# Projection units of two k tiles instead of one between the attention's steps

## The reference, cut to what matters

```python
for l in range(DEPTH):                       # DEPTH = 2
    hn = rmsnorm(h, norm_gain[l])
    proj = hn @ w_in[l]                      # 1040 x 1024 by 1024 x 4104
    dq, dk, dv, dg, fq, fk, fv, ff, fg = jnp.split(proj, split_points, axis=-1)
    dq, dk = partial_rope(dq, cos, sin), partial_rope(dk, cos, sin)
    do = diff_attention(dq, dk, dv, lam, chunk_ids)       # softmax(map 0) - lam * softmax(map 1)
    do = rmsnorm(do, subln_gain[l], SUBLN_EPS) * (1.0 - lam_init) * silu(dg)
    fo = forgetting_attention(fq, fk, fv, cum_logf, positions) * silu(fg)
    h = h + jnp.concatenate([do, fo], axis=-1) @ w_out[l]
```

## Time and profile before

| what | us |
|---|---|
| median of three runs | 2715.3 (2712.43 to 2716.8) |
| the profiled execution, its span | 2713.8, 2712.0 |
| TensorE busy | 2618.6 (97%) |
| VectorE, ScalarE, GpSimd busy | 1714.2, 1217.4, 468.4 |
| attention of layer 0 with its projections, about | 90 to 707 us of the span |
| the same of layer 1, about | 829 to 1492 us |

### The profile page before, as it was taken

How to read it: one execution, slowest core, us unless ns; L and a number is a source line. 1 busy time by engine, 2 the same in 40 slices (tenths; PEclk the granted TensorE clock), 3 DMA queues, 4 the chain that set the end, 5 groups by cost and what they waited for, 6 DMA issues and landing times.

```text
span 2712.0 us, 43192 instructions
## 1 busy us (share of the span) xinstructions
PE 2618.6 (97%) x16524; PEld 2278.8 (84%) x16524; DVE 1714.2 (63%) x3159; ACT 1217.4 (45%) x2433; POOL 468.4 (17%) x674
## 2 busy tenths in 40 slices
PE   6999999999999999999999999999998999999999
PEld 6888888888899878888888897888896788887887
DVE  5766665555535677665556476555437877778757
ACT  5444444444434344444344462223336555555444
POOL 2211312311002222344001133000013101011000
PEclk9999999999999999999999899999999999999999
DMA  4121567933311212699202423112232444444443
GB/s 148 54 74 65 159 159 189 231 102 106 134 55 65 69 65 78 178 248 236 82 26 83 132 79 109 40 47 101 94 101 87 124 125 129 120 125 155 173 154 136
DMA packets 219227, 314.23 MB, mean 116 GB/s; under 512 B 15478, under 2 KB 157494, under 8 KB 219022
## 3 DMA queue, kind: packets, MB, share of 16 engines
q0 software_dynamic: 50304, 151.30, 19.7%
q1 hardware_dynamic: 168720, 160.16, 18.6%
HBM read 267.26 MB, written 111.22 MB: 140 GB/s over the span
## 4 chain that ended last, share of the span: by engine, by line
PE 79%; DVE 7%; issue 6%; ACT 4%; DMA 2%; POOL 2%; ACTq 0%; DVEq 0%; SPq 0%; POOLq 0%
PE PS L1109 74%; PE PS L1118 4%; DMA T<-TMP 2%; DVE WL L2500 1%; DVE AL L2543 0%; DMA R<-in_k_fg 0%; POOL TMP L3500 0%; ACT top L1922 0%; DVE ST L2672 0%; DVE T L2648 0%; DVE top L2688 0%; POOL T L3497 0%; ACT TMP L1867 0%; DVE TMP L2655 0%; DVE top L2685 0%
## 5 line engine op out<-in xcount | busy, mean ns | idle before, releaser
L1109 PE MATMUL PS<-AH,WH 128*128 128x344 f32 (+2 forms) x2160 | 803.5, 372 | 21.8 <-DVE AL L2543 10.1
L1109 PE MATMUL PS<-AL,WH 128*128 128x344 f32 (+2 forms) x2160 | 756.8, 350 | 0.0
L1109 PE MATMUL PS<-AH,WL 128*128 128x344 f32 (+2 forms) x2160 | 756.7, 350 | 0.0
L1109 PEld LDWEIGHTS PS<-AH,WH 128*128 128x128 f32 x2160 | 408.9, 189 | 79.6 <-issue 20.8
L1109 PEld LDWEIGHTS PS<-AH,WL 128*128 128x128 f32 x2160 | 408.6, 189 | 35.8
L1109 PEld LDWEIGHTS PS<-AL,WH 128*128 128x128 f32 x2160 | 409.9, 190 | 32.0 <-issue 1.0
L1109 PE MATMUL PS<-WH,AH 128*128 128x256 f32 (+1 forms) x972 | 310.1, 319 | 7.4 <-DVE WL L2500 6.5
L1109 PE MATMUL PS<-WL,AH 128*128 128x256 f32 (+1 forms) x972 | 309.2, 318 | 0.0
L1109 PE MATMUL PS<-WH,AL 128*128 128x256 f32 (+1 forms) x972 | 309.0, 318 | 0.0
L2672 DVE TENSOR_REDUCE ST<-PS 128x1 f32<-128x784 f32 (+8 forms) x272 | 187.9, 732 | 132.6 <-PE PS L1109 132.0
L2500 DVE TENSOR_TENSOR WL<-W,WH 128x1024 fp32r<-128x1024 f32 x157 | 192.1, 1226 | 110.3 <-ACT WH L1745 110.2
(11 more groups left out here) (422 smaller groups left out, 4609.7 us busy)
## 6 DMA issues: line engine op xcount, KB each, us to landing
W<-in_k_w_in SPq DMA_DIRECT2D x66, 512.0 KB, 4.2
s_wt<-in_w_up POOLq DMA_DIRECT2D x96, 352.0 KB, 6.0
W<-in_w_ada SPq DMA_DIRECT2D x48, 512.0 KB, 5.2
s_wd<-in_w_down POOLq DMA_DIRECT2D x66, 256.0 KB, 7.1
W<-s_wt SPq DMA_DIRECT2D x64, 256.0 KB, 3.5
W<-in_w_in SPq DMA_DIRECT2D x28, 512.0 KB, 3.7
W<-in_w_up SPq DMA_DIRECT2D x52, 256.0 KB, 3.2
W<-in_w_out SPq DMA_DIRECT2D x24, 512.0 KB, 3.9
```

Of the source, the lines that this page charges most:

```text
L1109: return e.matmul(out, lhsT, rhs, start=start, stop=stop, skip_group_check=True)
```

## The change

A unit now holds two neighbouring k tiles, that is six matmuls of one chunk, and a chunk has four units instead of eight. The planner's cost of a unit is doubled, its last unit is the one with k = 6, and `step_unit` loops over the two tiles. Number, shapes and operands of all matmuls are as before; their order is worked out anew by the same planner.

```diff
@@ -484,7 +484,7 @@
         def chunk(g, kind, ci):
-            steps = [("unit", g, kind, ci, k) for k in range(KT)]
+            steps = [("unit", g, kind, ci, k) for k in range(0, KT, 2)]
@@ -540,7 +540,7 @@
                 if what == "unit":
-                    return 3 * (6.3 + 0.44 * cols_of(l, *st[1:3])[st[3]][1])
+                    return 6 * (6.3 + 0.44 * cols_of(l, *st[1:3])[st[3]][1])
@@ -569,7 +569,7 @@
-                    if k == KT - 1 and (kind == "v" or kind in "qk" and g < 4):
+                    if k == KT - 2 and (kind == "v" or kind in "qk" and g < 4):
                         need.append(0.0 if self.tmp[ci] is not None else None)
@@ -621,7 +621,7 @@
                         self.work = self.bank_of[key]
-                    if k == KT - 1:
+                    if k == KT - 2:
                         self.count += 1
@@ -1033,7 +1033,7 @@
-                elif st[0] == "unit" and st[4] == 7:
+                elif st[0] == "unit" and st[4] == KT - 2:
@@ -1191,9 +1191,10 @@
-                wv = slice(128 * k, 128 * k + 128)
-                m = mm3(e, bank(at_work[0])[:, 0:n], WH[:, t, wv], WL[:, t, wv], AH[:, k, c:c + n], AL[:, k, c:c + n], k == 0, k == KT - 1)
-                if k == KT - 1:
+                for kk in (k, k + 1):
+                    wv = slice(128 * kk, 128 * kk + 128)
+                    m = mm3(e, bank(at_work[0])[:, 0:n], WH[:, t, wv], WL[:, t, wv], AH[:, kk, c:c + n], AL[:, kk, c:c + n], kk == 0, kk == KT - 1)
+                if k == KT - 2:
                     m.then_inc(*gemm_mm.mark(key))
```

## The result

| | before | after |
|---|---|---|
| median of 20 runs each | 2711.2 us | 2716.9 us |
| ratio, 95% interval | | 1.0016 [1.001, 1.0022] |
| profiled execution, its span | 2713.8, 2712.0 | 2714.2, 2712.4 |
| attention of layer 0, first unit to output projection | 682.6 | 688.1 |
| the same of layer 1 | 664.6 | 660.4 |

A forecast was written before the change was run, and what follows sets the result against it. TensorE, busy 2618.6 of 2712.0 us, was taken to bound the kernel. Terms for switches, waits gone, waits added, layer 0's end and clock summed to -4.1 us: 2711.2 us from a 2715.3 median, own range 2706 to 2716, outer 2702 to 2721.

The forecast's parts named there:

- Part 1: Switches between kinds of TensorE work in the attention stages: 84 fewer starts of unit stretches, -1.4 us, from -3 to 0.
- rival that prices each passage at 0.088 us: Full entry price for each of the 84 fewer switches: -7.4 us instead of -1.4, giving 2705.2 us; chance 0.10.
- Part 2: Waits that go, in both attention stages: terms of -2.5, -1.2, -0.7 and -2.1 us.
- three waits of 0.85 us: First transposes of layer 0's heads 5 and 6 and layer 1's head 7, awaiting ScalarE's PSUM copies: gone, -2.5 us.
- long waits of layer 1: Scores waits at 1002.64 and 1083.89 us: one more unit ahead takes 0.6 us off each, -1.2 us.
- Part 3: Waits that come, before scores and at reused banks in both layers: +2.0, +1.3, +1.0 and +1.0 us.
- first bullet: Layer 0, head 1: block 4's scores, 17 transposes behind block 5's in a shared bank, wait 1.8 us; taken +2.0 us.
- the hold of TMP: Layer 0, head 1: k = 6 and 7 are held together until their TMP slice frees, so units can't fill the wait.
- Part 4: End of layer 0's attention: 3.1 us of work moves ahead of the last double unit; -1.0 us, from -4 to 0.
- Part 5: Layer 1's two long waits shrink, perhaps sparing the lower clock behind them; -0.5 us, from -3 to 0.
- the rival had it: Clock stays up at both places of layer 1 and at the end of layer 0: 2705 us; chance 0.10.
- slower by the grain: Steps wait longer inside double units, k = 6 held for TMP; six of sixteen heads hit: +9, 2724 us; chance 0.16.

The follow-up runs named there:

- experiment 9: Kernel before, with two middle steps swapped at 63 transpose, unit, transpose, unit places in TensorE's order alone: 2715.6 us, ratio 1.0012.
- experiment 4: Double units in layer 1 alone, layer 0 planned as before: 2710.3 us, ratio 0.9989 to the kernel before.
- experiment 3: Double units in layer 0 alone, layer 1 planned as before: 2719.4 us, ratio 1.0027 to the kernel before.
- experiment 5: After, replanned with PSUM bank 2 kept from units and small steps while layer 0's head 1 block 7 scores are next: 2710.9 us, ratio 0.9987.
- experiment 8: After, with k = 6 and k = 7 as single units and the other tiles in double units: 2726.4 us, ratio 1.0047 (5 runs).
- Experiment 10: The kernel with bank 2 kept for head 1's block 7, plus VectorE's low parts moved behind the last copies ending layer 0's attention: 2708.3 us, ratio 0.9982.
- experiment 1: After, with ScalarE's root step of head 0 moved behind head 1's block 6 exponentials, VectorE's following steps behind its normalisation: 2717.0 us, ratio 1.0015.
- experiment 2: After, with one double unit of head 2 moved ahead of head 1's block 5 scores on TensorE in layer 0: 2716.4 us, ratio 1.0017.
- experiment 7: Kernel before, single units, with layer 0's last v chunk of head 1 forced into bank 2 and the rest replanned: 2713.1 us, ratio 1.0003.
- experiment 6: After, with bank 2 kept from units and small steps whenever any head's block 7 scores are next, both layers: 2712.2 us, ratio 0.9994.

## Why the prediction was wrong, point by point

**Part 1 was right as far as it was tested.** TensorE's busy time moved by 0.8 us, within the 2 forecast, at the same mean clock (0.988), and experiment 9 excludes the rival that prices each passage at 0.088 us. TensorE in after shows the same trade: nine transposes (of V) in 0.90 us from 164.13, then 0.25 for the first matmul of a unit and 0.16 for the next.

**Part 2, mostly right, but others came.** The three waits of 0.85 us are gone, and so are the two of 0.34; 1.14 at 414.47, 0.84 at 1362.73 and 0.72 at 668.79 are new. The 1.17 at 181.65 is gone, and the like one of head 1 stayed (1.03 at 264.92), as said. Of the 1.83 ahead of the statistics, 1.34 came back before the scores at 969.63. The long waits of layer 1 shrank from 2.69 and 1.99 to 0.79 and 0.54, further than my 2.0 and 1.4, but 1.66 and, in place of 1.11, 1.48 stand some 9 us ahead of them: a chain that is late twice instead of once. And 2.72 at 1481.54 stands where 0.81 stood; the clock is low behind it until 1488 us, for the most part in the output projection, which the 660.4 us don't count. TensorE's idle time in layer 1 fell only from 18.6 to 17.6 us (rows with waits over 0.25 us added up), and yet the stage is 4.1 us shorter in the profiled execution and 3.0 by experiment 4. Part of this is the clock: from 990 to 1010 us it was 0.91 before and is 1.00 after. How much each part gives stays open.

**Part 3 has the step that failed**, its first bullet, "Taken: +2.0 us". Without part 1 the terms of layer 0 came to about -0.3 us (-1.7 - 1.2 - 0.7 + 2.0 + 1.3 + 1.0 - 1.0), and experiment 3 measures +7.3. I priced the wait before block 4 by its own release (1.09 us came) and took the start of the chain as given. The chain itself was 4 to 11 us late, and the place costs 5.0 us of idle time and about 3 to 6 us by the clock (estimated: half of low stretches of 6.8 to 13.7 us, less the time that was idle anyway). It showed in the order: TensorE's plan has `scores_1_7` 15 steps behind `scores_0_8`. I looked at which steps stand between two scores, and not at which banks they hold. Nor did I count ScalarE's root step, 4.7 us without a break, as something queued ahead of a late exponential, or VectorE's 2.59 us of waiting for the rotation's DMA ahead of block 7's normalising. The reason that I gave for the lack of filler, the hold of TMP, is refuted by experiments 5 and 8. Heads 5 and 6 cost 0.69 and 0.65 where 0.6 each was said, plus 0.43 each before a small transpose. Block 2 of heads 1 and 2 was to wait 1.0 us longer and waits 1.2 less.

**Part 4 had the right reason and too large a gain.** Both waits are as they were (2.21 and 2.71 against 2.26 and 2.62), since VectorE's low parts came along. The low stretch is 6.8 us long instead of 10.2. Experiment 10 shows what the reason was worth once acted on.

**Part 5**: in after the clock stayed up at layer 1's two places, as the rival had it, but in three of the five experiments that share after's plan of layer 1 (1, 4 and 10, not 2 and 5) it fell some 9 us ahead of the first of them, for 3.4 us. So that it stayed up in after was in part luck, and the rival had no room for head 1.

The rival "slower by the grain" had the sign and named the place, but it wanted six places and the hold of TMP. One place did, by another mechanism: the grain changed the moment at which a chunk drew its bank. It was no property of the double units by themselves: experiment 5 has them all and wins 0.13%.

## What to carry to other kernels

A planner that draws buffers by longest free will sooner or later give a long holder the one buffer that the critical step needs next; compare, between the old plan and the new, the start of each critical step and who holds its buffer, before pricing any wait behind it. Where a chain runs late, look for the longest unbroken work in the queue of each engine that it passes, and for steps ahead of it that wait for a DMA; moving the unbroken work by itself only moved the wait (experiment 1). And undo a change stage by stage before judging it: here a gain of 3.0 us lay under a loss of 7.3.

## What the runs showed of the hardware

- Behind waits of TensorE of 2.4 to 3.7 us at this place the granted clock fell to its lower level for 3.4 (experiment 7) to 13.7 us (experiment 3), and for 6.8 us in after, whose order in layer 0 is that of experiment 3.
- The spread from run to run is for the most part one of the clock. Of the 20 runs of after, the shortest (2711.5 us) had a mean granted clock of 0.989 and the longest (2720.6 us) one of 0.985; over all 20, time and mean clock have a correlation of -0.92. Estimated from these, 0.004 of the span is 22 us more at half speed, so 11 us; the two differ by 9. Over all 20 the mean clock is 0.9867, and 0.9879 over the 35 runs of before beside experiments 1 to 4; by the same reckoning that is up to 3 us of the 4.3 lost. By this estimate most of the loss is paid through the clock that falls behind the waits.
- The same scores step in layer 1 waited 1.48 us in experiment 2, 1.65 in experiment 5 and 1.66 in after (996.38), with the clock staying at its upper level behind it, and 1.87, 2.00, 2.06 and 2.18 us in experiments 6, 4, 1 and 10, where a low stretch of 3.4 us followed each time. TensorE and the window in experiment 4:

```profile
991.45 0.45 PE L1116 MATMUL PS<-KH,QH 64*128 64x400 f32 x2 [2.00 <-ACT top L1930]
```

```profile
990.00:1000.00 10.00, 8.55 (x46) 6.40 (x47) 8.02 (x18) 5.64 (x12) 3.41 (x4) 0.83 0.01 4
```

- At the lower clock (1.2 GHz) 17 transposes took 3.88 us; at the upper (2.4 GHz) give 0.107 each, 1.8 us.
- A passage from transposes to a unit and back costs about 3 ns net in the kernel before, as medians over the attention stages with units of 344 columns: between transposes 109 ns from start to start, from the last transpose to the unit 28, the unit's first matmul 242 and the following 158; 242 - 158 - (109 - 28) = 3. The prediction had 12 from a few rows.
